# Queries and keys of the windowed heads turned in the projection and stored turned, bias tables built ahead of the global stage

## The chip, the core and the metric

The kernel runs on one core of a Trainium2 chip as one program. The metric is the device time of the whole program in microseconds, as the median of several runs; lower is better. TensorE (PE) multiplies and transposes, VectorE (DVE), ScalarE (ACT) and GpSimd (POOL) do the rest, and SyncE (SP) issues most transfers between memory and the core's SBUF. The engines run their own instruction lists and wait for each other on semaphores.

## What is computed

One encoder layer on x of 2048 rows by 1024, all in float32. Half of the 16 heads (A) attend to the whole sequence, half (B) to a band of 128 positions on each side, with a bias from a table and a learned sink logit. Each half has 8 query heads and 2 key heads of width 64.

```python
h = rmsnorm(x, g_pre_mix)
qa, ka, va, qb, kb, vb = split(h @ w_in)          # 512, 128, 128, 512, 128, 128 columns
out_a = softmax(rope(rmsnorm(qa)) @ rope(rmsnorm(ka)).T / 8) @ va
# for each block of 128 queries of B, over the 384 keys around it:
s = qb @ kb.T / 8 + rel_table[t5_bucket(rel)]     # -1e30 outside the band or the sequence
m = max(max(s), sink)
out_b = exp(s - m) / (sum(exp(s - m)) + exp(sink - m)) @ vb
x = x + rmsnorm(concat(out_a, out_b) @ w_o, g_post_mix)
x = x + rmsnorm(relu(rmsnorm(x, g_pre_ffn) @ w_up) ** 2 @ w_down, g_post_ffn)
```

## The kernel before

Six stages follow each other, and no instruction of one begins before all engines have left the one before: `project`, `attend_global`, `attend_window`, `mix_heads`, `ffn_up`, `ffn_down`. The change touches the first three. Inside a stage every engine's instructions are written out by hand in the order in which it runs them; that order, the waits on semaphores and the order of issues on each engine's DMA queue set what runs when. Nearly every value is carried as a rounded high part and a rest, so that a product of two of them takes two or three passes; a query or key of width 64 therefore fills 128 columns, high and low.

`project` walks 16 tiles of 128 rows. For a tile, TensorE does three chunks of 512 columns (`chunk`, 24 products each), turns the next tile's normalised x behind the first (`turn`), and behind the third turns the ten heads of A of the tile before (`turn_qk`, eight query and two key heads, 128 x 128 each) into one PSUM tile, `qk_ps`. ScalarE evacuates the chunks, copies the turned heads to SBUF (`keep_turned`, L282) and issues stores (`store_qk`, L275 to L277); SP stores the turned heads (`store_turned`). The heads of B are split on VectorE into `q_out` and `k_out` and stored as they are, unturned, to `q_split` and `k_split`. The loop runs over pairs of tiles with the first and the last pair written out (`sweep`).

`attend_global` has 32 blocks (8 heads by 4 chunks of 512 queries) of 8 units each, fully written out. Its start loads queries and keys on SP's queue, computes the row maxima of block 0 in eight pairs of products and three pairs of block 1, and then begins the scores (L766).

`attend_window` has 32 steps, n = 16 query blocks by 2 groups of 4 heads. Its start builds what the steps need. SP loads constants, then the keys in 4 chunks, then the denominators of the global stage (L902, read by VectorE behind the wait of L1099), then queries. TensorE makes an 8 x 512 row of biases (L1119); it goes to memory and comes back as 128 shifted copies (L943, L946, on POOL's queue), and eight products with a flipped identity (L1139), each copied by VectorE (L1069), make the tables `bias`. TensorE also turns the keys, 64 transposes (L1127). In step n it does the four scores of step n + 1 (L1161, L1162, two PSUM banks taken in turn), turns the eight query operands of step n + 2 (L1150, L1151, copied by ScalarE in L1013 and L1014), turns the probabilities (L1169, 12 transposes), folds an output and weighs the values. VectorE adds bias and takes the maximum for each of four heads (L1078), with a one-column copy that nothing reads ahead of each (L1077), and subtracts the rounded probabilities from the exact ones (L1087) after ScalarE has evicted them (L1028). The steps are a `sweep` with two pairs written out in front.

## Time and profile before

| | |
|---|---|
| median of 3 runs | 2890.35 us (2888.19 to 2890.84) |
| the profiled execution | 2890.22 us, of it 2888.6 us span |
| projection | from 0 to about 338.7 us |
| global stage | to about 1051 us |
| window stage | to about 1292 us |
| rest | to 2888.6 us |
| busy, share of the span | PE 94%, DVE 63%, ACT 49%, POOL 28% |
| mean granted clock of TensorE | 0.972 of full speed |

The page of the profile gives busy times and shares of one execution. A timeline row is one instruction or a merged run of equal ones: start, duration, engine, line, operation, output and inputs, shape, count, and in brackets how long the engine had been idle and what ended that. An engine name with a q behind it is the engine's sequencer issuing a transfer; its duration is that of the issue, not of the transfer. TensorE's durations include the time through the array, so rows of one run overlap, and the pace is read from start to start.

### The profile page before, as it was taken

What the parts mean: (1) busy time and instruction counts of PE and PEld (TensorE: products, weight loads), DVE (VectorE), ACT (ScalarE), POOL (GpSimd) and SP (SyncE); (2) the same over time, 40 slices, a digit from 0 to 9 for tenths busy, and PEclk for the clock granted to TensorE, in tenths of its full rate; (3) what the DMA queues carried; (4) which work ended last, traced back from release to release, by engine and by line L of the source; (5) the groups of instructions that cost most, each with busy time, mean ns of one, the idle gap of its engine ahead of it and who ended that gap; (6) DMA issues with size and microseconds to landing.
All of it is one profiled execution on the core that took longest, in us unless ns stands there. A gap on an engine that the chain in (4) does not pass through costs nothing. (4 is left out here: it accounts for less than half of the span.)

```text
span 2888.6 us, 36041 instructions
## 1 busy us (share of the span) xinstructions
PE 2705.4 (94%) x12274; PEld 2185.6 (76%) x12274; DVE 1827.9 (63%) x2503; ACT 1429.2 (49%) x2122; POOL 803.3 (28%) x603
## 2 busy tenths in 40 slices
PE   7999599999999978988995999999998999999998
PEld 5888467777777747976874888788886888888887
DVE  5666499999999947865556666675653343343433
ACT  3222177777777747973334544554443333233332
POOL 1111178888888854541110000000000000000000
PEclk9999799999999989998997999999999999999999
DMA  5333421111111122327876333533325445355442
GB/s 181 107 108 102 122 67 30 31 34 28 35 30 32 23 75 70 84 67 218 207 202 216 124 117 97 209 107 100 114 92 189 171 172 182 121 196 179 172 172 98
DMA packets 295611, 338.16 MB, mean 117 GB/s; under 512 B 73059, under 2 KB 219635, under 8 KB 293292
## 3 DMA queue, kind: packets, MB, share of 16 engines
q1 hardware_dynamic: 269980, 317.92, 35.7%
q10 hardware_dynamic: 23552, 13.64, 1.5%
q0 software_dynamic: 1936, 4.74, 0.6%
q8 instruction: 84, 1.38, 0.2%
q14 instruction: 59, 0.48, 0.0%
HBM read 234.10 MB, written 97.86 MB: 115 GB/s over the span
## 5 line engine op out<-in xcount | busy, mean ns | idle before, releaser
L126 PE MATMUL d_pr<-d_w_hi,d_s_hi 128*128 128x512 f32 x1024 | 399.7, 390 | 11.6 <-DVE d_s_lo L1872 11.6
L1871 DVE TENSOR_TENSOR d_w_lo<-d_w_raw,d_w_hi 128x1024 fp32r<-128x1024 f32 x128 | 156.8, 1225 | 386.2 <-ACT d_s_hi L1848 382.3
L127 PE MATMUL d_pr<-d_w_lo,d_s_hi 128*128 128x512 f32 x1024 | 399.5, 390 | 0.0
L128 PE MATMUL d_pr<-d_w_hi,d_s_lo 128*128 128x512 f32 x1024 | 399.3, 390 | 0.0
L644 POOL TENSOR_TENSOR p_sum<-p_sum,p_hi 128x1024 f32<-128x1024 f32 x160 | 383.3, 2396 | 37.0 <-issue 19.7
L126 PE MATMUL u_pr<-u_t_hi,u_w_hi 128*128 128x512 f32 x896 | 351.2, 392 | 32.3 <-DVE u_t_lo L1687 31.9
L127 PE MATMUL u_pr<-u_t_lo,u_w_hi 128*128 128x512 f32 x896 | 350.1, 391 | 0.0
L128 PE MATMUL u_pr<-u_t_hi,u_w_lo 128*128 128x512 f32 x896 | 350.1, 391 | 0.0
L676 ACT ACTIVATE p_hi<-s_ps 128x1024 fp32r<-128x1024 f32 x256 | 263.3, 1028 | 157.0 <-PE s_ps L767 155.7
L720 DVE TENSOR_TENSOR p_lo<-s_ps,p_hi 128x1024 fp32r<-128x1024 f32 x256 | 312.5, 1221 | 29.5 <-ACT s_ps L677 22.3
L704 DVE TENSOR_REDUCE part_max<-m_ps 128x1 f32<-128x1024 f32 x251 | 304.6, 1214 | 33.1 <-PE m_ps L749 32.9
L1846 ACT ACTIVATE d_w_hi<-d_w_raw 128x1024 fp32r<-128x1024 f32 x128 | 135.6, 1060 | 271.0 <-PE d_pr L128 181.3
L677 ACT ACTIVATE s_ps<-s_ps 128x1024 f32<-128x1024 f32 x256 | 261.4, 1021 | 0.0
L766 PE MATMUL s_ps<-q_all,kt 128*128 128x512 f32 x512 | 219.1, 428 | 18.3 <-DVE p_lo L720 18.2
L126 PEld LDWEIGHTS d_pr<-d_w_hi,d_s_hi 128*128 128x128 f32 x1024 | 192.9, 188 | 52.2 <-DVE d_s_lo L1872 12.1
L128 PEld LDWEIGHTS d_pr<-d_w_hi,d_s_lo 128*128 128x128 f32 x1024 | 193.0, 188 | 40.2
L127 PEld LDWEIGHTS d_pr<-d_w_lo,d_s_hi 128*128 128x128 f32 x1024 | 193.0, 188 | 40.0
L126 PEld LDWEIGHTS u_pr<-u_t_hi,u_w_hi 128*128 128x128 f32 x896 | 169.2, 189 | 70.4 <-issue 34.4
L1630 ACT ACTIVATE u_pr<-u_pr 128x512 f32<-128x512 f32 x128 | 74.5, 582 | 273.4 <-DVE u_pr L1716 126.7
L767 PE MATMUL s_ps<-q_max,kt 65*128 65x512 f32 x512 | 203.9, 398 | 0.0
L1839 POOL TENSOR_TENSOR d_rstd<-d_var,d_half 128x1 f32<-128x1 f32 x16 | 8.8, 550 | 699.7 <-DVE d_var L1879 699.7
L127 PEld LDWEIGHTS u_pr<-u_t_lo,u_w_hi 128*128 128x128 f32 x896 | 169.3, 189 | 35.2
(219 smaller groups left out, 5384.5 us busy)
## 6 DMA issues: line engine op xcount, KB each, us to landing
d_w_raw<-in_w_ffn_down SPq DMA_DIRECT2D x128, 512.0 KB, 3.8
u_w_raw<-in_w_ffn_up SPq DMA_DIRECT2D x32, 1024.0 KB, 6.0
act_blocks<-u_s_out SPq DMA_DIRECT2D x128, 256.0 KB, 6.2
d_s_lo<-act_blocks SPq DMA_DIRECT2D x128, 256.0 KB, 2.7
u_t_lo<-h_blocks SPq DMA_DIRECT2D x14, 1024.0 KB, 10.9
x_in<-in_x SPq DMA_DIRECT2D x16, 512.0 KB, 4.3
q_split<-q_out ACTq DMA_DIRECT2D x16, 512.0 KB, 3.3
q_turned<-w_raw SPq DMA_DIRECT2D x16, 512.0 KB, 3.4
```

Of the source, the lines that this page charges most:

```text
L126: nc.tensor.matmul(out, stat_hi, mov_hi, start=first, stop=False)
L127: nc.tensor.matmul(out, stat_hi, mov_lo, start=False, stop=False)
L128: return nc.tensor.matmul(out, stat_lo, mov_hi, start=False, stop=last)
L644: nc.gpsimd.tensor_tensor(p_sum[:, s], first, p_hi[:, (UNITS * n + u) % SLOTS].bitcast(F32), ALU.add).then_inc(added, 1)
L676: nc.scalar.activation(p_hi[:, slot], scored, ACT.Exp).then_inc(p_hi_ready, 1)
L677: nc.scalar.activation(scored, scored, ACT.Exp).then_inc(probs_ready, 1)
L704: nc.vector.tensor_reduce(part_max[:, m // (PAIRS // QT), m % (PAIRS // QT):m % (PAIRS // QT) + 1], products.rearrange("p b c -> p (b c)") ...
L720: nc.vector.tensor_tensor(p_lo[:, slot], scored, p_hi[:, slot].bitcast(F32), ALU.subtract).then_inc(p_lo_ready, 1)
L766: nc.tensor.matmul(bank, kt[:, g, 0, keys], q_all[:, n % QS], start=True, stop=False)
L767: last = nc.tensor.matmul(bank, kt[0:HD + 1, g, 1, keys], q_max[0:HD + 1, n % QS], start=False, stop=True)
L1846: nc.scalar.activation(w_hi[:, n % SLOTS], w_raw[:, n % RAW], ACT.Copy)
L1871: nc.vector.tensor_tensor(w_lo[:, n % SLOTS], w_raw[:, n % RAW], w_hi[:, n % SLOTS].bitcast(F32), ALU.subtract)
```

## The change

In `project`, the heads of B go into `qkb_out`, of the same form as `qk_out`, and are turned, copied and stored like those of A, by a second call of `turn_qk`, `keep_turned` and `store_turned`; the turned tensors in memory have all 16 heads. `attend_global` gets the making of the bias row and tables, now with the two output banks, and stores the tables to memory. `attend_window` loads turned keys and queries straight into the operand tiles (queries in four slots), and the tables from memory; the turns, their copies, and the one-column copy are gone, and its steps are all written out.

```diff
+        qkb_out = sb("qkb_out", [P, 2, 10, 2 * HD])
+        qkb_t = sb("qkb_t", [P, 2, 10, P])
...
             def store_turned(t, s):
-                sp.wait_ge(qk_kept, t + 1)
-                sp.dma_start(q_cols[t], qk_t[:, s, 0:8]).then_inc(qk_stored[s], 16)
-                sp.dma_start(k_cols[t], qk_t[:, s, 8:10]).then_inc(qk_stored[s], 16)
+                for b, turned in enumerate((qk_t, qkb_t)):
+                    sp.wait_ge(qk_kept, 2 * t + b + 1)
+                    sp.dma_start(q_cols[t][:, 8 * b:8 * b + 8], turned[:, s, 0:8]).then_inc(qk_stored[s], 16)
+                    sp.dma_start(k_cols[t][:, NG * b:NG * b + NG], turned[:, s, 8:10]).then_inc(qk_stored[s], 16)
...
                 act.wait_ge(post_done, t + 1)
-                act.dma_start(scratch["q"].rearrange("(h t) p c -> t p h c", t=NT)[t], q_out[:, s]).then_inc(stored[s], 16)
-                act.dma_start(scratch["k"][t], k_out[:, s]).then_inc(stored[s], 16)
                 act.dma_start(scratch["v_glob"][t], v_out[:, s]).then_inc(stored[s], 16)
...
+                if not (isinstance(t, int) and t < 2):
+                    keep_turned(t - 2, s, p - 1, 1)
                 evacuate(t, s, p, 1)
...
             for s in range(2):
-                keep_turned(NT - 2 + s, s, NT // 2 - 1)
+                for b in range(2):
+                    keep_turned(NT - 2 + s, s, NT // 2 - 1, b)
...
-            def turn_qk(t, s):
+            def turn_qk(t, s, b):
                 pe.wait_ge(post_done, t + 1)
-                at_least(pe, qk_kept, t)
+                at_least(pe, qk_kept, 2 * t + b)
                 for h in range(10):
-                    last = nc.tensor.transpose(qk_ps[:, h], qk_out[:, s, h], ident[:])
+                    last = nc.tensor.transpose(qk_ps[:, h], (qk_out, qkb_out)[b][:, s, h], ident[:])
...
+                if not (isinstance(t, int) and t < 2):
+                    turn_qk(t - 2, s, 1)
                 chunk(t, s, 1)
                 chunk(t, s, 2)
-                turn_qk(t - 1, 1 - s)
+                turn_qk(t - 1, 1 - s, 0)
 
             sweep(pe, NT // 2, tile)
-            turn_qk(NT - 1, 1)
+            turn_qk(NT - 2, 0, 1)
+            for b in range(2):
+                turn_qk(NT - 1, 1, b)
...
             load_q(2)
+            sp.wait_ge(row_ready, 1)
+            sp.dma_start(scratch["bias_row"], bias_row[:]).then_inc(row_moved, 16)
+            sp.wait_ge(row_moved, 16)
+            rows = scratch["bias_row"]
+            sp.dma_start(bias_rev[:], bass.AP(tensor=rows.tensor, offset=rows.offset, ap=[[1, P], [512, 8], [1, SPAN]])).then_inc(row_moved, 16)
             place_max(0)
...
+            pe.wait_ge(row_moved, 32)
+            pe.wait_ge(row_ready, 1)
+            for h in range(8):
+                at_least(pe, bias_ready, h - 1)
+                nc.tensor.matmul((oa_ps, ob_ps)[h % 2][:, 0:SPAN], flip[:], bias_rev[:, h], start=True, stop=True).then_inc(bias_product, 1)
+            pe.wait_ge(bias_ready, 8)
+            pe.wait_ge(filled, 4)
             for n in range(TOTAL):
...
+            load_q(0)
+            load_k(0)
+            sp.dma_start(sink[:], a["sink_b"].to_broadcast([P, 8])).then_inc(const_in, 16)
+            load_bias(0)
             sp.dma_start(ident[:], a["ident"]).then_inc(const_in, 16)
...
+            load_q(1)
+            load_bias(1)
+            load_q(2)
+            load_k(1)
+            load_k(2)
+            load_k(3)
             for j in range(2):
                 sp.dma_start(den[:, j], scratch["den"][j].rearrange("n (t q) -> (n t) q", q=P)).then_inc(den_loaded, 16)
...
-                    nc.vector.tensor_copy(mark[:, h:h + 1], sink[:, head:head + 1])
                     nc.vector.tensor_tensor_reduce(probs[:, s, h], s_ps[:, h % 2, 0:SPAN], bias[:, head], 1.0,
...
                         scores(n + 1, 1 - s, b + s, h)
-                    if h == 0 and not known(n, TOTAL - 2):
-                        turn_q(n + 2, s, b + 1)
                     if h:
                         turn_probs(n, s, h - 1)
```

How the instructions stand. TensorE in the projection's loop, around the turn of the next x; `xt` is the turned x, `qk_ps` the PSUM tile of the turned heads, `pj` the chunks. Before:

```order
L128 MATMUL pj<-w_hi,xt_lo 128x512
L421 REGISTER_ALU
L424 MATMUL xt<-ident,xn 128x128 x8
L59 REGISTER_ALU
L126 MATMUL pj<-w_hi,xt_hi 128x512
L127 MATMUL pj<-w_lo,xt_hi 128x512
```

and now:

```order
L110 MATMUL pj<-w_hi,xt_lo 128x512
L407 REGISTER_ALU
L410 MATMUL xt<-ident,xn 128x128 x8
L59 ISA
L426 MATMUL qk_ps<-ident,qkb_out 128x128 x10
L59 REGISTER_ALU
L108 MATMUL pj<-w_hi,xt_hi 128x512
L109 MATMUL pj<-w_lo,xt_hi 128x512
```

A second group of ten transposes stands between the turned x and the second chunk. SP at the start of the window stage, before:

```order
L895 DMA w_ident<-in_ident 128x128
L896 DMA flip<-in_flip 128x128
L897 DMA onehot<-in_bucket_onehot 33x512
L898 DMA table<-in_rel_bias 32x8
L899 DMA sink<-in_sink_b 128x8
L94 DMA wk_in<-k_split 128x4x128 x8
L902 DMA w_g_den<-den 128x128 x2
L907 DMA wq_in<-q_split 128x4x128 x2
```

and now (`wq_all`, `wq_one` and `wkt` are the operand tiles of queries and keys, `w_g_den` the denominators):

```order
L927 DMA bias<-bias_tables 128x1536
L923 DMA wq_all<-q_turned 128x4x128
L923 DMA wq_one<-q_turned 64x4x128
L914 DMA wkt<-k_turned 64x2x512 x2
L915 DMA wkt<-k_turned 64x2x512
L914 DMA wkt<-k_turned 64x2x512 x2
L915 DMA wkt<-k_turned 64x2x512
L914 DMA wkt<-k_turned 64x2x512 x2
L915 DMA wkt<-k_turned 64x2x512
L941 DMA w_g_den<-den 128x128 x2
L943 DMA rden<-w_g_rden 128x128
```

Ahead of this piece stand eight issues more: query block 0 (two), the first keys (three), the sinks, the first half of the tables and the identity, and behind those the two of query block 1. The denominators, once behind 13 issues of constants and unturned keys, now stand behind 22 of keys, queries and tables. TensorE at the start of the global stage, now, from the last three pairs of products for the maxima (`m_ps`) to the first scores (`s_ps`); before, the scores followed the row of `m_ps` directly:

```order
L766 MATMUL m_ps<-kt,q_all 128x512 x6
L826 MATMUL oa_ps<-bias_rev,flip 128x384
L826 MATMUL ob_ps<-bias_rev,flip 128x384
L826 MATMUL oa_ps<-bias_rev,flip 128x384
L826 MATMUL ob_ps<-bias_rev,flip 128x384
L826 MATMUL oa_ps<-bias_rev,flip 128x384
L826 MATMUL ob_ps<-bias_rev,flip 128x384
L826 MATMUL oa_ps<-bias_rev,flip 128x384
L826 MATMUL ob_ps<-bias_rev,flip 128x384
L783 MATMUL s_ps<-q_all,kt 128x512
```

## Rows read from the trace of the kernel before

**Rows 1.** Busy time by stretch: us, then PE, PEld, DVE, ACT, POOL, clock, DMA share, GB/s.

```profile
39.00:341.00 302.00, 279.42 (x1352) 233.85 (x1352) 187.64 (x348) 78.77 (x137) 54.29 (x31) 0.96 0.35 106
...
1100.00:1293.00 193.00, 184.87 (x1295) 164.18 (x1293) 158.05 (x457) 167.30 (x401) 103.68 (x187) 1.00 0.29 74
```

**Rows 2.** Timeline of TensorE in the projection's loop, around one group of ten transposes.

```profile
300.19 0.39 PE L128 MATMUL pj<-w_hi,xt_lo 128*128 128x512 f32 x1
...
300.42 1.25 PE L440 MATMUL qk_ps<-ident,qk_out 128*128 128x128 f32 x10
...
301.43 0.48 PE L126 MATMUL pj<-w_hi,xt_hi 128*128 128x512 f32 x1
```

**Rows 3.** Timeline of the end of the projection: ScalarE's issues and copies, TensorE's last turns.

```profile
327.15 0.39 ACTq L275 DMA_DIRECT2D q_split<-q_out  x1
...
328.21 1.16 ACTq L277 DMA_DIRECT2D v_glob<-v_out  x1
329.47 1.24 ACT L282 ACTIVATE w_raw<-qk_ps 128x1280 f32<-128x1280 f32 x1 [10.74 <-issue]
...
330.85 2.37 PE L440 MATMUL qk_ps<-ident,qk_out 128*128 128x128 f32 x10 [11.72 <-ACT w_raw L282]
...
333.25 1.24 ACT L282 ACTIVATE w_raw<-qk_ps 128x1280 f32<-128x1280 f32 x1 [2.55 <-PE qk_ps L440]
```

**Rows 4.** Timeline of the start of the global stage: SP's issue, TensorE.

```profile
343.62 7.96 SPq L549 DMA_DIRECT2D q_all<-q_turned  x1
...
363.97 1.19 PE L749 MATMUL m_ps<-kt,q_all 128*128 128x512 f32 x2 [1.41 <-DVE part_max L704]
...
364.96 0.63 PE L766 MATMUL s_ps<-q_all,kt 128*128 128x512 f32 x1
```

**Rows 5.** Table transfer (page, DMA issues) and timeline of the table products and copies.

```profile
bias_rev<-bias_row POOLq DMA_DIRECT2D x1, 1536.0 KB, 7.0
...
1075.62 6.14 PE L1139 MATMUL w_ptp<-bias_rev,flip 128*128 128x384 f32 x16
...
1081.15 1.20 DVE L1069 COPY bias<-w_ptp 128x384 f32<-128x384 f32 x2 [0.36 <-PE w_ptp L1139]
```

**Rows 6.** Timeline of the start of the window stage.

```profile
1051.89 0.36 SPq L895 DMA_DIRECT2D w_ident<-in_ident  x1
...
1090.59 0.28 DVE L1100 TENSOR_TENSOR w_g_den_sum<-w_g_den 128x128 f32<-128x128 f32 x1
...
1091.83 0.61 DVE L1078 CUSTOM_DVE_ANT_0 wprobs<-w_s,bias,sink 128x384 f32<-128x384 f32 x1
...
1100.36 1.46 ACT L1028 ACTIVATE w_pt_hi<-w_ptp 128x1536 fp32r<-128x1536 f32 x1 [1.99 <-PE w_ptp L1169]
```

**Rows 7.** Busy time by stretch, columns as in Rows 1, while loads run.

```profile
340.00:342.00 2.00, 0.00 (x0) 0.00 (x0) 0.00 (x0) 0.00 (x0) 2.00 (x1) 0.50 0.79 168
...
344.00:346.00 2.00, 0.00 (x0) 0.00 (x0) 0.00 (x0) 0.00 (x0) 0.99 (x5) 0.50 1.01 225
...
1060.00:1062.00 2.00, 2.00 (x11) 1.77 (x10) 0.50 (x2) 0.60 (x1) 0.13 (x1) 0.50 1.19 297
...
1068.00:1070.00 2.00, 1.50 (x12) 1.02 (x10) 1.03 (x2) 0.60 (x1) 0.00 (x0) 1.00 0.98 369
```

**Rows 8.** Timeline of the last steps of the window stage, VectorE and TensorE.

```profile
1267.43 1.76 DVE L1087 TENSOR_TENSOR w_pt_lo<-w_ptp,w_pt_hi 128x1536 fp32r<-128x1536 f32 x1
...
1273.35 1.76 DVE L1087 TENSOR_TENSOR w_pt_lo<-w_ptp,w_pt_hi 128x1536 fp32r<-128x1536 f32 x1 [0.22 <-ACT w_pt_hi L1028]
1275.03 0.14 DVE L1077 COPY w_mark<-sink 128x1 f32<-128x1 f32 x1
1275.09 0.61 DVE L1078 CUSTOM_DVE_ANT_0 wprobs<-w_s,bias,sink 128x384 f32<-128x384 f32 x1
...
1279.23 1.76 DVE L1087 TENSOR_TENSOR w_pt_lo<-w_ptp,w_pt_hi 128x1536 fp32r<-128x1536 f32 x1 [0.22 <-ACT w_pt_hi L1028]
...
1275.17 0.55 PE L1169 MATMUL w_ptp<-w_ident,wprobs 128*128 128x128 f32 x3 [0.35 <-DVE w_pt_lo L1087]
```

More of the change, by code:

```diff
@@ new lines, in load_q, with load_bias @@
+            def load_q(n):
+                at_least(sp, scores_done, GRP * (n - QS + 1))
+                b, g = n // NG, n % NG
+                heads = slice(8 + GRP * g, 8 + GRP * (g + 1))
+                dest = (q_all[:, n % QS], q_one[0:HD, n % QS])
+                for tile, rows in zip(dest, (slice(0, 2 * HD), slice(HD, 2 * HD))):
+                    sp.dma_start(tile.bitcast(F32).rearrange("p (h c) -> p h c", h=GRP), q_cols[b][rows, heads]).then_inc(q_loaded[n % QS], 16)
+            def load_bias(g):
+                heads = slice(GRP * g, GRP * (g + 1))
+                sp.dma_start(bias[:, heads], scratch["bias"][:, heads]).then_inc(bias_in[g], 16)
@@ L909, in _ @@
-            for g in range(NG):
-                load_q(0, g)
             sp.wait_ge(den_inverted, 1)
@@ L919, in step @@
             def step(n, g, b):
-                if not known(n, TOTAL - 2):
-                    load_q(b + 1, g)
+                if n + 3 < TOTAL:
+                    load_q(n + 3)
                 if not (isinstance(n, int) and n < 4):
                     store(n - 4, b - 2, g)
-            sweep(sp, NT, step, 2)
+            every(sp, NT, step)
             for n in range(TOTAL - 4, TOTAL):
@@ L994, in step @@
                     load_v(b + 1, s)
-            sweep(pool, NT, step, 2)
+            every(pool, NT, step)
             denominator(TOTAL - 1, 1)
@@ L1046, in step @@
                     exponentials(n + 1, 1 - s)
-            sweep(act, NT, step, 2)
+            every(act, NT, step)
             keep_o(TOTAL - 2, 0)
@@ L1109, in step @@
                 low(n, s)
-            sweep(dve, NT, step, 2)
+            every(dve, NT, step)
             finish(TOTAL - 2, 0, NT - 1)
@@ L1212, in step @@
                     weigh(n - 1, 1 - s)
-            sweep(pe, NT, step, 2)
+            every(pe, NT, step)
             turn_o(TOTAL - 2, 0)
```

227 lines of the change are left out of this document (79 added, 148 removed).

## The prediction

> **What bounds the kernel now.** I read the busy time of the stages first, then the timeline at the seams between them, then one step of the window stage. From 39 to 341 us, the projection, TensorE is busy 279.42 of 302.00 us, and in the window stage 184.87 of 193.00 [rows 1]; VectorE and ScalarE have room in the first and less of it in the second. In the projection the reader should see ten transposes standing between two runs of products with no idle time ahead of them: they start at 300.42, the next product at 301.43 and it takes 0.48 instead of 0.39 [rows 2]. So one group of ten costs 1.01 + 0.09 = 1.10 us of a chain that never stops. At the seams TensorE stands still: at the end of the projection it waits for ScalarE's copies [rows 3], at the start of the window stage for keys, tables and one query load [rows 6]. In the running window step the question is whether TensorE or a chain through three engines sets the period; this decides whether taking its query turns away is worth anything.
>
> **Part 1, the projection's loop: +15.4 us.** Each tile gets a second group of ten transposes. For tiles 0 to 13 these stand behind the first chunk of a later tile, 14 groups at 1.10 us [rows 2], and nothing in that loop idles TensorE, so all of it lies on the path. What goes away there (two of ScalarE's three stores a tile) and what comes (a second copy of 1.24 us a tile, two more issues on SP) lies beside it: ScalarE is busy 78.77 of 302 us [rows 1]. Bounds: 0 if some wait absorbed it, for which no row speaks, and 15.4.
>
> **Part 2, the projection's end: +6.5 us.** Before, ScalarE issues its last three stores, the last from 328.21, then copies (329.47), TensorE turns the last tile (330.85, 2.37 us at the lower clock), and ScalarE copies again (333.25 to 334.49) [rows 3]. One copy-and-turn round is 333.25 - 329.47 = 3.78 us. After the change one store is left of three; it is issued about 1.06 us earlier (328.21 - 327.15, the time at which the first one stands in the rows), so the copies begin at 328.4. But there are now four copies with three turns between them, each waiting for the other because the turned heads share one PSUM tile: 328.4 + 3 x 3.78 + 1.24 = 341.0 against 334.5. If the clock came back in the later rounds, a turn would take the 1.25 us of [rows 2] and the end would be about 2.2 us earlier: bounds 4.3 and 6.5. I take 6.5, since TensorE idles 1.4 of every 3.8 us there.
>
> **Part 3, the global stage's start: +7.8 us.** The small product and its copy lie under the loading of the keys, for which TensorE waits anyway. The 1.5 MB table transfer does not: SP can issue the row only behind the third query load, whose issue lasts from 343.62 to 351.58 [rows 4], it must then wait for the row to land, and the transfer took 7.0 us to land before [rows 5]. That puts the tables in SBUF at about 364 to 366. TensorE finishes its eleven pairs of products at 363.97 + 1.19 = 365.16 [rows 4], so up to here it is nearly hidden. The eight products and copies are not: from 1075.62 to 1081.15 + 1.20 = 1082.35 they took 6.7 us [rows 5], they now stand ahead of the first scores, and their first copy must wait for VectorE's reduction of the last pair, for which TensorE waits 1.41 us ahead of the product at 363.97 [rows 4]; I take 1.2 us. 365.2 + 1.2 + 5.9 = 372.3 and 0.4 us to the first score's start, against 364.96: +7.8. Bounds: +5.5 if the clock comes back during the tables and spares the slow first products that follow now; +11 if the row or the tables land 3 us later. The store of the finished tables and SP's wait for them come when the next query load is still many units away from being needed; nothing for them.
>
> **Part 4, the window stage's start: -17.5 us.** The stage begins at 1051.89, and the first eviction of turned probabilities, which needs a whole first step, starts at 1100.36 [rows 6]. Key turns, table products and query turns between them disappear. What is late next? The first scores need about 2 MB and should start near 1061. But VectorE, after the first block's four heads, waits for the softmax denominators (L1099), and their load now stands on SP's queue behind every key, bias and early query load: 3.15 MB of keys, 1.18 MB of queries, 1.57 MB of tables, 0.2 MB of small ones. I take rates from [rows 7]: 225 GB/s while keys went to 64 partitions, 297 for 512-byte pieces, 369 for the tables. 14.0 + 4.0 + 4.3 + 0.7 = 23.0 us, with some 2 us until the engines are full and 0.3 at the end: 1077.2. From the sum of the denominators to the end of the first head of block 1 it takes 1091.83 + 0.61 - 1090.59 = 1.85 us [rows 6]: 1079.0. From there to the eviction: in a running step the distance from a head's copy to the next VectorE subtraction is 1279.23 - 1275.03 = 4.20 us [rows 8]; without 0.7 for the head and 1.5 for the eviction 2.0 us remain. About 1.7 of that is TensorE's (nine transposes at 0.10 and four products of 384 columns at three quarters of 0.23, both from [rows 2]), which doubles at the lower clock: 3.7 to 3.8. Eviction at 1082.8, 17.5 us earlier. Bounds: everything at 369 GB/s gives 6.8 us more gain, keys at 168 (while the first ones of the global stage came in, [rows 7]) 4.8 us less. The wait for denominators is the new wait here; behind it on VectorE stands all of block 1.
>
> **Part 5, the window's steps: -3.0 us.** TensorE looks full, and eight query turns a step go. But the kernel before contains a step without them. The subtractions stand at 1267.43, 1273.35 and 1279.23 [rows 8]: 5.92 us with turns, 5.88 us without, and in the second TensorE waits 0.35 us for the subtraction (row at 1275.17). So the period belongs to the chain subtraction - first head on VectorE - third scores - turns of the probabilities - eviction - subtraction. The removed copy of one column adds 1275.09 - 1275.03 = 0.06 us to that chain once a step, since the copy stands ahead of the first head. 5.82 us a step, 0.10 less, 30 steps: 3.0 us. Bounds: 1.2 us (5.88) to what a TensorE-bound step would give, the first rival. ScalarE's two query copies (1.1 us a step) fall into its idle time before the eviction; their cover was that idle time, so nothing is won.
>
> **Sum.** 15.4 + 6.5 + 7.8 - 17.5 - 3.0 = +9.2 us. The profiled execution took 2890.22 us (span 2888.6), 0.13 below the median of 2890.35; forecast 2899.4 us.
>
> **The rivals.** *TensorE sets the window's period (faster).* Then each step loses its eight turns, 8 x 0.11 = 0.87 us with the delay of the product behind them [rows 2], 26 us instead of 3: 2899.4 - 23 = 2876. For it: TensorE's 184.87 of 193 us, which looks like the bound. Against it: the 5.88 us step. It decides if the chain through VectorE can start earlier once turns are gone; that needs more than 0.3 us a step. *The loads come at the full rate.* The denominators at 1070.4, the clock returning at the projection's end: 2899.4 - 6.8 - 2 = 2891, no difference that can be told. For it: 369 GB/s for tables in [rows 7]; against it: the keys' 225. *The loads are slow.* Keys at 168 GB/s and the global stage's tables 3 us late: 2899.4 + 4.8 + 3 = 2907. For it: many issues ahead of the denominators, and SP's 7.96 us for one issue [rows 4]. *The added turns hide.* If the projection had slack that the rows don't show, Part 1 is zero: 2884.
>
> The Trainium skill bears on the second rival ("DMA: Bandwidth & Descriptors", sections Specifications and "Anatomy of one DMA"): about 2.0 us fixed plus bytes over the rate, with some 358 GB/s as one core's share of memory. By that, 5.97 MB are there 18.7 us after the issue, at 1070.6, and the sum would be 2893. The trace doesn't agree with one rate for all: 369 GB/s is above that limit, and 225 far below it.
>
> **How the numbers follow.** Forecast 0.50, steps bound by TensorE 0.11, full-rate loads 0.22, slow loads 0.12, hidden turns 0.05. The forecast's own bounds are 2893 to 2905. The range 2888 to 2908 leaves out the first and last rival on the fast side (0.16) and a little above. A measurement of this kernel can tell about 0.2% (5.8 us) from no change. Slower by more than that, above 2896.1: 0.62 (the forecast and the slow loads). Within: 0.22. Faster, below 2884.6: 0.16.
>
> **What would show it.** In the profile after: a tile of the projection 1.10 us longer than before; four copies from the transposes' PSUM tile at the projection's end, 3.8 us apart; eight table products ahead of the first scores of the global stage and those scores some 8 us further from the stage's start; VectorE idle for about 10 us before the denominators' sum, ended by their DMA; the subtractions of the window stage 5.8 us apart. I would be wrong first of all if these stand 5.1 us apart, or if VectorE doesn't wait for the denominators.

## The result and the profile after

The changed kernel takes 2906.03 us (median of 5 runs, 2902.15 to 2907.04) against 2890.35 us (2888.19 to 2892.11) before: ratio 1.0051, with a 95% interval of 1.0037 to 1.0066. Slower by 15.7 us, where 9.2 were forecast. Between the two profiled executions the cost came in at 29.8 us (29.7 forecast) and the gain at 16.0 us (20.5 forecast); 2.9 us more lie in stages that the change doesn't touch.

SyncE's first load of each stage divides the executions. Its timeline before, for the two places that the rows ahead don't show:

```profile
338.76 0.36 SPq L549 DMA_DIRECT2D q_all<-q_turned  x1
...
1292.71 0.36 SPq L1295 DMA_DIRECT2D m_ident<-in_ident  x1
```

and after, for the global, the window and the mix stage:

```profile
359.29 0.36 SPq L548 DMA_DIRECT2D q_all<-q_turned  x1
...
1081.74 0.41 SPq L923 DMA_DIRECT2D wq_all<-q_turned  x1
...
1306.52 0.35 SPq L1245 DMA_DIRECT2D m_ident<-in_ident  x1
```

The reader takes the stages' lengths from these starts, [rows 6] and the spans (2888.6 and 2905.3 us). The same reading for every kernel of this study, in us ("times" are medians; the ratio is to the kernel before on the same chip):

| kernel | projection | global | window | the rest | span | time | ratio |
|---|---|---|---|---|---|---|---|
| before | 338.8 | 713.1 | 240.8 | 1595.9 | 2888.6 | 2890.35 | |
| after | 359.3 | 722.4 | 224.8 | 1598.8 | 2905.3 | 2906.03 | 1.0051 |
| after_again | 359.6 | 724.5 | 226.8 | 1594.1 | 2905.0 | 2906.47 | 1.0048 |
| before_extra_turns | 353.9 | 713.9 | 240.5 | 1597.3 | 2905.6 | 2907.22 | 1.0051 |
| tail_banks | 352.2 | 722.4 | 225.7 | 1593.9 | 2894.1 | 2895.67 | 1.0019 |
| late_tables | 360.7 | 720.5 | 224.7 | 1594.4 | 2900.3 | 2902.16 | 1.0039 |
| den_early | 359.8 | 724.6 | 213.4 | 1592.3 | 2890.1 | 2891.76 | 1.0007 |
| keys_later | 358.7 | 723.9 | 218.1 | 1593.9 | 2894.6 | 2898.18 | 1.0026 |
| window_filler | 358.9 | 724.0 | 225.8 | 1595.6 | 2904.4 | 2906.31 | 1.0051 |
| after_with_mark | 359.3 | 724.2 | 226.3 | 1592.7 | 2902.5 | 2903.91 | 1.0051 |
| three_slots | 359.1 | 720.8 | 216.8 | 1595.8 | 2892.4 | 2897.94 | 1.0030 |
| turns_together | 359.2 | 723.4 | 205.4 | 1596.7 | 2884.6 | 2885.84 | 0.9975 |
| combined | 352.9 | 719.8 | 199.5 | 1593.7 | 2865.8 | 2865.66 | 0.9911 |
| combined_keys_later | 352.9 | 717.7 | 202.8 | 1595.7 | 2869.2 | 2866.47 | 0.9919 |

From before to after: projection +20.5, global stage +9.3, window stage -16.0, rest +2.9, together 16.7 us between the profiled executions. The rest runs the same instructions in all rows of the table and lies anywhere from 1592.3 to 1598.8: it is scatter. A single stage's row is good to some 2 us, which is why the experiments below are read at the place that their edit touches, and in the whole time only second. The mean over all executions that run the same instructions in a stage (nine of the projection and of the global stage after, four of the window stage after; one of the projection before and two of the other two stages) gives +20.6, +9.8 and -15.2 us, together 15.2: the difference of the medians, with nothing left for the rest.

**The projection.** The timeline of TensorE in the loop, the rows that answer to [rows 2]:

```profile
300.99 0.39 PE L110 MATMUL pj<-w_hi,xt_lo 128*128 128x512 f32 x1
...
302.10 1.25 PE L426 MATMUL qk_ps<-ident,qkb_out 128*128 128x128 f32 x10
303.11 0.48 PE L108 MATMUL pj<-w_hi,xt_hi 128*128 128x512 f32 x1
```

The new group of ten takes 1.01 us to the next product and delays that by 0.09, as the old one did. Its end, by VectorE's last subtraction, ScalarE's store and copies, and one of TensorE's turns (to be set beside [rows 3]):

```profile
341.65 0.29 DVE L353 TENSOR_TENSOR qk_out<-rot,qk_out 128x128 f32<-128x128 f32 x1
...
341.97 0.34 ACTq L259 DMA_DIRECT2D v_glob<-w_raw  x1
342.41 1.24 ACT L264 ACTIVATE w_raw<-qk_ps 128x1280 f32<-128x1280 f32 x1 [8.88 <-DVE qk_out L353]
346.19 1.24 ACT L264 ACTIVATE qkb_t<-qk_ps 128x1280 f32<-128x1280 f32 x1 [2.55 <-PE qk_ps L426]
349.98 1.24 ACT L264 ACTIVATE w_raw<-qk_ps 128x1280 f32<-128x1280 f32 x1 [2.55 <-PE qk_ps L426]
353.77 1.24 ACT L264 ACTIVATE qkb_t<-qk_ps 128x1280 f32<-128x1280 f32 x1 [2.55 <-PE qk_ps L426]
...
347.58 2.37 PE L426 MATMUL qk_ps<-ident,qk_out 128*128 128x128 f32 x10 [1.42 <-ACT qkb_t L264]
```

Four copies 3.78 us apart, each waiting for a turn, each turn for the copy before it. The last copy ends at 355.01, 20.5 us later than at 334.49.

**The global stage's start.** TensorE's last pair of maxima products, the first and fifth table product, VectorE's last table copy and the first scores, and beside them the busy time with the granted clock (columns as in [rows 1]):

```profile
384.99 1.19 PE L766 MATMUL m_ps<-kt,q_all 128*128 128x512 f32 x2 [1.41 <-DVE part_max L716]
386.00 1.65 PE L826 MATMUL oa_ps<-bias_rev,flip 128*128 128x384 f32 x2
387.44 1.49 PE L826 MATMUL ob_ps<-bias_rev,flip 128*128 128x384 f32 x2
...
391.28 0.82 PE L826 MATMUL oa_ps<-bias_rev,flip 128*128 128x384 f32 x2
...
394.62 0.56 DVE L742 COPY g_bias<-ob_ps 128x384 f32<-128x384 f32 x1 [0.36 <-PE ob_ps L826]
...
395.23 0.50 PE L783 MATMUL s_ps<-q_all,kt 128*128 128x512 f32 x1 [0.65 <-DVE g_bias L742]
...
384.00:390.00 6.00, 5.01 (x8) 2.59 (x9) 3.18 (x4) 0.00 (x0) 0.00 (x0) 0.50 0.11 22
```

The first scores stand 35.9 us behind the stage's first load, 26.2 before (364.96 in [rows 4] less 338.76). The tables' stretch, 386.00 to 395.18, is 9.2 us long.

**The window stage's start.** VectorE's sum of the denominators, ScalarE's first eviction, the first two subtractions, and the busy time while the loads run and in the first step:

```profile
1109.82 0.29 DVE L1088 TENSOR_TENSOR w_g_den_sum<-w_g_den 128x128 f32<-128x128 f32 x1 [10.97 <-DMA w_g_den<-den]
...
1115.16 1.45 ACT L1029 ACTIVATE w_pt_hi<-w_ptp 128x1536 fp32r<-128x1536 f32 x1 [13.68 <-PE w_ptp L1123]
...
1116.65 1.76 DVE L1075 TENSOR_TENSOR w_pt_lo<-w_ptp,w_pt_hi 128x1536 fp32r<-128x1536 f32 x1 [1.79 <-ACT w_pt_hi L1029]
...
1123.75 1.76 DVE L1075 TENSOR_TENSOR w_pt_lo<-w_ptp,w_pt_hi 128x1536 fp32r<-128x1536 f32 x1 [1.53 <-ACT w_pt_hi L1029]
...
1084.00:1108.00 24.00, 5.72 (x15) 3.81 (x15) 7.78 (x14) 2.60 (x9) 2.50 (x5) 0.50 1.00 251
1110.00:1123.00 13.00, 8.73 (x38) 7.68 (x39) 7.71 (x21) 4.67 (x11) 4.01 (x8) 0.68 0.46 115
```

The new wait is where it was forecast, 10.97 us for the denominators. The eviction comes 33.4 us after the stage's first load, 48.5 before [rows 6]; the second subtraction 7.10 us after the first.

**The steps.** One step of the running stage, TensorE's turn, ScalarE's eviction, VectorE's subtractions, and the busy time of 24 steps:

```profile
1240.46 1.76 DVE L1075 TENSOR_TENSOR w_pt_lo<-w_ptp,w_pt_hi 128x1536 fp32r<-128x1536 f32 x1 [0.22 <-ACT w_pt_hi L1029]
...
1242.27 0.55 PE L1123 MATMUL w_ptp<-w_ident,wprobs 128*128 128x128 f32 x3 [0.35 <-DVE w_pt_lo L1075]
...
1244.81 1.45 ACT L1029 ACTIVATE w_pt_hi<-w_ptp 128x1536 fp32r<-128x1536 f32 x1 [1.42 <-PE w_ptp L1123]
...
1246.29 1.76 DVE L1075 TENSOR_TENSOR w_pt_lo<-w_ptp,w_pt_hi 128x1536 fp32r<-128x1536 f32 x1 [0.22 <-ACT w_pt_hi L1029]
...
1130.00:1270.00 140.00, 131.63 (x817) 106.77 (x816) 112.20 (x265) 105.97 (x266) 80.33 (x144) 1.00 0.41 108
```

5.83 us a step, with TensorE waiting for the subtraction in each. Every engine has idle time: the step is a ring of waits, not a full engine. The same stretch of the kernel before:

```profile
1130.00:1270.00 140.00, 140.00 (x995) 126.34 (x994) 121.06 (x353) 127.89 (x310) 77.99 (x142) 1.00 0.31 81
```

There TensorE never stops. Its own instructions fill the 5.92 us of a step, and neither a product nor a weight load of it waits for another engine in these 140 us. The step without turns in [rows 8] takes 5.88 us and has a wait of 0.35 us.

### The profile page after: what moved, and what is told of

Read it like the earlier page. It is cut to its first block and busy times, and to the rows that moved or that the text cites. A ratio compares the mean times of both kernels' runs of the same rounds, so it can differ in the third digit from the quotient of the medians.

```text
span 2905.3 us, 34682 instructions
## 1 busy us (share of the span) xinstructions
PE 2700.0 (93%) x12114; PEld 2168.7 (75%) x12114; DVE 1816.2 (63%) x2367; ACT 1411.0 (49%) x2066; POOL 797.7 (27%) x598
## 5 line engine op out<-in xcount | busy, mean ns | idle before, releaser
L110 PEld LDWEIGHTS u_pr<-u_t_hi,u_w_lo 128*128 128x128 f32 x896 | 169.1, 189 | 35.5
```

Of the source, the lines that this page charges most:

```text
L110: return nc.tensor.matmul(out, stat_lo, mov_hi, start=False, stop=last)
```

## The experiments

The theory is the forecast's: five separate terms, of which the projection's are TensorE's time and one shared PSUM tile, the window's start is the denominators behind the other loads, and the window's steps are a chain. The rivals are named with each run.

**The base again.** No edit.

> The kernel after, unchanged, as the base of the other three of this group on the same chip. The stages behind the window stage, which the change doesn't touch, took from 1592.3 to 1598.8 us in six profiled executions, and 1598.8 in the one of after. Theory (2.9 of the 16.7 us by which the two profiled executions differ are this scatter, not the change): the median lies at 2902 to 2905 us, ratio to before 1.004 to 1.005, and the part in front of the mix stage's first load is again 13.8 us longer than before's, within 1 us. Rival (the change costs the later stages 3 us): 2905 to 2908 us.

2906.47 us (2903.96 to 2907.16), ratio 1.0048 (1.0034 to 1.0061). The time was not lower, and the mix stage's first load stood 18.2 us later than before's, not 13.8: in this execution the scatter lay in the global and window stages and the rest was short (1594.1). So both numbers of the theory missed. The time lies in the rival's range, but not by its mechanism: the later stages cost nothing by themselves. One pair of profiles doesn't split 15 us to the microsecond. The difference of 15 to 16 us is firm.

**The projection's loop by itself**, in the kernel before:

```
+                if not (isinstance(t, int) and t < 2):
+                    at_least(pe, qk_kept, t - 1)
+                    for h in range(10):
+                        nc.tensor.transpose(qk_ps[:, 10 + h % 2], ident[:], ident[:])
                 chunk(t, s, 1)
```

> The kernel before, with ten transposes of the identity, into two unused slots of the turned heads' PSUM tile, in each of tiles 2 to 15 of the projection, where the kernel after turns the local heads; nothing else changes: no copies, no stores, no queues. Theory (the loop's cost is TensorE's time alone): VectorE's last split comes 14 to 15.4 us later than in before and the kernel takes 14 to 16 us more, 2904 to 2906. Rival (the turns hide, and the projection of after is longer for its copies and stores): 0 to 4 us more.

2907.22 us, ratio 1.0051 (1.0038 to 1.0065), 15.9 us more. VectorE's last subtraction, which stood at 326.83 in the kernel before:

```profile
342.01 0.29 DVE L368 TENSOR_TENSOR qk_out<-rot,qk_out 128x128 f32<-128x128 f32 x1
```

15.2 us for 14 groups, 1.08 each, with no copy, store or queue changed. The loop's cost is TensorE's time alone, and the rival that the turns hide has fallen.

**The projection's end on two PSUM tiles:**

```
-            turn_qk(NT - 2, 0, 1)
-            for b in range(2):
-                turn_qk(NT - 1, 1, b)
+            pj_heads = pj[:].rearrange("p b (h c) -> p (b h) c", c=P)
+            pe.wait_ge(evacuated, 3 * NT)
+            turn_qk(NT - 2, 0, 1, pj_heads)
+            turn_qk(NT - 1, 1, 0, qk_ps)
+            turn_qk(NT - 1, 1, 1, pj_heads)
```

(Cut: `turn_qk` gets the tile as an argument, and its wait for ScalarE's copies is one copy looser.) ScalarE copies both groups of tile 14 ahead of its last store.

> The kernel after, with the projection's last turns alternating between two PSUM tiles (the turned heads' and that of the projection's products, free by then), and ScalarE's copies of tile 14 ahead of its last store. Theory (the end is longer because four copies and three turns wait for each other over one PSUM tile, 3.78 us a round): the four copies no longer stand 3.8 us apart, ScalarE's last one ends about 348 instead of 355.0, and the kernel takes 6 to 7 us less, about 2899. Rival (the low clock and the stores' landing set the end): the copies move together, but the global stage starts less than 3 us earlier, 2903 or more.

2895.67 us, ratio 1.0019 (1.0010 to 1.0028). ScalarE's last two copies:

```profile
344.31 1.24 ACT L265 ACTIVATE w_raw<-qk_ps 128x1280 f32<-128x1280 f32 x1 [7.58 <-PE qk_ps L429]
346.37 1.24 ACT L265 ACTIVATE qkb_t<-pj 128x1280 f32<-128x1280 f32 x1 [0.82 <-PE pj L429]
```

The last ends at 347.61 and the global stage begins at 352.2, 7.1 us earlier than in after, as the theory said; the time fell by 10.4, 3 more than the edit explains. The turns were as slow as before (2.3 to 2.4 us, the lower clock), so overlapping them with the copies is enough to shorten the end; what a full clock would give there wasn't run.

**The tables at the global stage's end:**

```
+                    if n == TOTAL - 1:
+                        if u == 0:
+                            pe.wait_ge(row_moved, 32)
+                            pe.wait_ge(max_reduced, PAIRS * TOTAL)
+                        at_least(pe, bias_ready, u - 1)
+                        nc.tensor.matmul(m_ps[:, u % 2, 0:SPAN], flip[:], bias_rev[:, u], start=True, stop=True).then_inc(bias_product, 1)
```

> The kernel after, with the bias tables' eight products and copies placed one by one in the eight units of the global stage's last iteration, where the PSUM tile of the maxima is free and TensorE waits 0.5 us in every second unit, the table transfer issued in the third iteration, and the small product behind the first eleven pairs of products. Theory (the tables cost 9.7 us at the start: 1.0 by a late first product and 8.7 ahead of the first scores): the first scores come 9 us earlier against the stage's start, of which the small product there takes 0.5 to 1; in the last iteration the eight products cost 0 to 5 us; in all 4 to 8 us less, about 2900. Rival (what the tables took was given back at once by a warm clock, so that it was nearly free): less than 2 us, 2904 or more.

2902.16 us (2899.56 to 2902.72), ratio 1.0039 (1.0026 to 1.0053): 3.9 us less, below the 4 to 8 expected and above the rival's 2. At the start the small product and the first scores, and near the end one of the eight products:

```profile
387.83 1.87 PE L822 MATMUL ob_ps<-onehot,table 33*8 33x512 f32 x2
389.63 0.79 PE L784 MATMUL s_ps<-q_all,kt 128*128 128x512 f32 x1
...
1060.03 0.81 PE L836 MATMUL m_ps<-bias_rev,flip 128*128 128x384 f32 x2
1060.38 0.92 PE L799 MATMUL oa_ps<-p_hi,v 128*128 128x512 f32 x2
```

The first scores come 29.0 us after the stage's first load instead of 35.9. The small product, 1.80 us from start to start at the lower clock, now stands in their way. Each table product costs 0.35 us and 0.29 us at the product behind it, 5 us in eight units. The tables are thus worth 7 us at the start, 9 with the small product, and TensorE had little room for them elsewhere.

**The denominators' load on ScalarE's queue:**

```
@@ SyncE, behind load_k(3)
-            for j in range(2):
-                sp.dma_start(den[:, j], ...).then_inc(den_loaded, 16)
@@ ScalarE, ahead of exponentials(0, 0)
+            for j in range(2):
+                act.dma_start(den[:, j], ...).then_inc(den_loaded, 16)
```

> The kernel after, with the two loads of the global stage's denominators issued by ScalarE as its first instructions of the window stage instead of by SyncE behind 22 other issues. Theory (the denominators' load is the new wait of the window stage's start): VectorE's wait of 10.97 us ahead of their sum falls to under 1 us, the first eviction of turned probabilities comes 9 to 11 us earlier against the stage's first load, and the kernel takes about 2896 us against 2906 (ratio to before about 1.002). Rival (the second block's queries and tables, which stand in the same queue, come almost as late): a new wait takes over most of it, the gain is 0 to 4 us, 2902 to 2906.

2891.76 us, ratio 1.0007 (0.9998 to 1.0016). VectorE's sum and the first eviction:

```profile
1101.08 0.29 DVE L1088 TENSOR_TENSOR w_g_den_sum<-w_g_den 128x128 f32<-128x128 f32 x1
...
1106.03 1.45 ACT L1027 ACTIVATE w_pt_hi<-w_ptp 128x1536 fp32r<-128x1536 f32 x1 [2.23 <-PE w_ptp L1123]
```

No wait ahead of the sum is left, and the eviction comes 21.7 us after the stage's first load (1084.34) instead of 33.4. The window stage is 213.4 us long, 11 to 13 shorter than in the four kernels whose window stage is that of after. The time fell by 14.3 us by the medians (12.7 by the ratios), where 10 were expected. The gain at the place of the edit, 11.7 us, is the wait of 10.97; it alone was worth most of what the change lost.

**Fewer bytes ahead of the denominators,** which stay on SyncE's queue:

```
             load_k(1)
-            load_k(2)
-            load_k(3)
@@ step
+                if n in (2, 5):
+                    load_k(2 + n // 5)
```

> The kernel after, with the last two of the four chunks of window keys loaded in steps 2 and 5 of the window stage instead of at its start; the denominators stay on SyncE's queue, behind the rest. Theory (the wait for the denominators is the bytes ahead of them over the rate of this stretch, 6.27 MB in 24 us, 261 GB/s): 1.57 MB less put them 6.0 us earlier, the wait ahead of their sum is 5 to 6 us instead of 11 to 12, and the kernel takes 5 to 6.5 us less than after, about 2900. Rival (they wait for SyncE's issues, 0.6 us each, and for the landing, not for bytes): six issues less put them 3.6 us earlier, about 2902.5.

2898.18 us, ratio 1.0026 (1.0016 to 1.0036), 8 us less than after and a little more than the 5 to 6.5 expected.

```profile
1103.82 0.29 DVE L1088 TENSOR_TENSOR w_g_den_sum<-w_g_den 128x128 f32<-128x128 f32 x1 [4.12 <-DMA w_g_den<-den]
```

The sum stands 21.2 us behind the stage's first load (1082.61), 6.9 us earlier than in after, and 6.9 less is waited. (The row of after gives 251 GB/s for 1084 to 1108 and not the 261 of the expectation, so 1.57 MB are 6.3 us.) The rival's 3.6 us, issues alone, is too little. The trace of after says the same: SyncE issued the denominators' loads from 1097.93 on, 11.9 us before the sum could start.

**TensorE's turns put back** into the window steps, as transposes of the identity:

```
+                    if h == 0:
+                        for k in range(2 * GRP):
+                            nc.tensor.transpose(tb_ps[:, k % GRP], ident[:], ident[:])
```

> The kernel after, with eight transposes of the identity into a free PSUM bank in each of the window stage's steps, where the kernel before turned its queries. Theory (a chain through VectorE and ScalarE sets the step, and TensorE's turns fall mostly into its wait for the subtraction): the subtractions stand 5.83 to 5.92 us apart instead of 5.83, in all 0 to 3 us more than after. Rival (TensorE sets the step): 0.87 us a step more, 6.7 us apart, 26 us more in all.

2906.31 us. Two subtractions and the filler between them:

```profile
1242.11 1.76 DVE L1076 TENSOR_TENSOR w_pt_lo<-w_ptp,w_pt_hi 128x1536 fp32r<-128x1536 f32 x1 [0.22 <-ACT w_pt_hi L1030]
...
1248.01 1.76 DVE L1076 TENSOR_TENSOR w_pt_lo<-w_ptp,w_pt_hi 128x1536 fp32r<-128x1536 f32 x1 [0.22 <-ACT w_pt_hi L1030]
...
1243.06 1.04 PE L1159 MATMUL w_tb<-w_ident 128*128 128x128 f32 x8
```

5.90 us a step: eight turns of TensorE cost 0.07 us, not 0.87. But they also fill TensorE, as they did before. The busy time in the running stage, and between the first two subtractions:

```profile
1130.00:1270.00 140.00, 140.00 (x1000) 126.50 (x998) 115.17 (x261) 104.58 (x263) 78.97 (x142) 1.00 0.40 106
...
1118.00:1124.00 6.00, 4.58 (x29) 3.53 (x28) 4.25 (x10) 4.10 (x11) 2.48 (x5) 1.00 0.42 106
```

So there are two bounds next to each other. With eight turns TensorE's own work is 5.90 us; without them it is about 5.03 (5.90 less 0.80 from the first turn's start to the next product and 0.07 by which that is slower, an estimate), and the ring of 5.83 sets the step. The rival added the turns' 0.87 us to the ring's 5.83; they belong on TensorE's own 5.03. The turns do something else too: the first two subtractions stand 5.83 us apart here (1118.35 and 1124.18) at the full clock, and 7.10 to 7.44 us in the four kernels whose window stage is that of after. So the turns cost 1.8 us over the later steps and gave 1.3 to 1.6 back in the first.

**The one-column copies put back,** ahead of each head:

```
+                    nc.vector.tensor_copy(mark[:, h:h + 1], sink[:, head:head + 1])
```

> The kernel after, with the copy of one column ahead of each head on VectorE put back. Theory (one of a step's four copies stands in the chain that sets the step, 0.06 us): the subtractions stand 5.89 us apart instead of 5.83, in all 2 us more than after (2908), which the time can hardly tell and the rows can. Rival (all four copies stand in it, since VectorE is full): 6.0 to 6.1 us apart, 5 to 8 us more.

2903.91 us (2903.31 to 2909.05), no difference from after by time. The subtractions stand 5.89 to 5.90 us apart, 0.06 more, and TensorE still waits in each step: one of the four copies is in the ring. The kernel before had both, a ring of 5.89 us with the copies and turns that fill TensorE for 5.90 or more; its 5.92 are the larger of the two and not their sum.

**A third PSUM slot for the scores:**

```
-        s_ps = ps("w_s", [P, 2, NB])
+        s_ps = ps("w_s", [P, 3, NB])
@@ scores; the slot is (GRP * n + h) % 3
-                at_least(pe, biased, GRP * n + h - 1)
+                at_least(pe, biased, GRP * n + h - 2)
```

> The kernel after, with three PSUM slots instead of two for a block's scores, in the bank that the query turns left free. Theory (a chain sets the window's period of 5.83 us: subtraction, first head on VectorE, third head's scores, turns of the probabilities, eviction, subtraction; TensorE does not bound it): the third scores no longer wait for the first head, the chain loses 0.3 to 0.5 us, the subtractions stand 5.3 to 5.5 us apart and the kernel takes 10 to 16 us less, 2890 to 2896. Rival (TensorE's work or the clock sets the period): it stays at 5.8 us and the time at 2906.

2897.94 us, ratio 1.0030 (1.0018 to 1.0042), 8.1 us less, short of the 10 to 16 expected. The subtractions stand 5.58 us apart, short of the 5.3 to 5.5 expected, and TensorE still waits 0.36 us for each: the wait for the first head is gone (the third scores start 0.30 us behind the first turn, 0.54 in after), but two heads' scores still stand between the turns.

**The turns together,** in the kernel three_slots:

```
-                for h in range(GRP):
+                for h in range(GRP - 1):
                     if not known(n, TOTAL - 1):
                         scores(n + 1, 1 - s, b + s, h)
-                    if h:
-                        turn_probs(n, s, h - 1)
-                turn_probs(n, s, GRP - 1)
+                for h in range(GRP):
+                    turn_probs(n, s, h)
+                if not known(n, TOTAL - 1):
+                    scores(n + 1, 1 - s, b + s, GRP - 1)
```

> The kernel three_slots, with TensorE's order in a window step changed: three heads' scores, then all four heads' turns of probabilities, then the last head's scores, instead of scores and turns in alternation. Theory (in three_slots the chain of subtraction, turns and two scores between them, eviction and subtraction sets the step of 5.58 us; without the two scores it is 4.9, and TensorE's own work of 5.22 us sets it): the subtractions stand 5.2 to 5.3 us apart, 9 to 12 us less than three_slots, 2886 to 2889 us. Rival (VectorE is full): 5.5 us or more, less than 3 us gained.

2885.84 us, ratio 0.9975 (0.9966 to 0.9984). Subtractions, and the busy time of the running stage:

```profile
1242.08 1.75 DVE L1075 TENSOR_TENSOR w_pt_lo<-w_ptp,w_pt_hi 128x1536 fp32r<-128x1536 f32 x1
...
1247.32 1.75 DVE L1075 TENSOR_TENSOR w_pt_lo<-w_ptp,w_pt_hi 128x1536 fp32r<-128x1536 f32 x1
...
1130.00:1270.00 140.00, 139.35 (x905) 120.57 (x904) 118.54 (x291) 120.26 (x291) 88.05 (x159) 1.00 0.42 113
```

5.24 us between these two, 5.27 in the mean of the stage. No product of TensorE waits any longer, but it isn't quite a full engine: in each step a weight load waits 0.25 us for ScalarE's last exponential, and ScalarE 0.65 us for GpSimd. Only now does it pay to have taken the queries' turns away, since with them TensorE's own work was 5.90 us a step (this order with the turns wasn't run). VectorE is busy 118.54 of 140 us: the rival has fallen.

**All of them.** The edits of tail_banks, late_tables, den_early and turns_together, with late_tables' small product ahead of the last three pairs of products.

> The edits of den_early, tail_banks, late_tables and turns_together in one kernel; of late_tables the small product stands one place earlier, ahead of the last three pairs of products, where TensorE waits 2.7 us for VectorE. Theory (each removes a separate stretch of the path, so their gains add): the projection's end 7 us earlier, first scores of the global stage 7 to 8.5 us earlier against its start with 5 us given back in its last iteration, no wait for the denominators (11 us), window steps of 5.25 us; 2906 - 7 - 3 - 11 - 20 = 2865 us, ratio to before 0.991, range 2861 to 2870. Rival (what one edit frees another takes back: turns_together already evicts the first block ahead of VectorE's wait, and a window start bound by the keys' loads): 2872 us or more.

2865.66 us (2861.32 to 2868.97), ratio 0.9911 (0.9896 to 0.9926): the fastest kernel here, 25 us below the one before. Against after the projection lost 6.4 us, the global stage 2.7, the window stage 25.3, where the sum had 31: here the rival was right in part. That the time still came out at the 2865 expected is luck: 5.1 us of the difference of the two profiled executions lie in the untouched rest, where after had its longest value. A new wait has taken 6 us: the second and third subtraction stand 11.39 us apart. TensorE at the third block's scores, and GpSimd's issue of a value load and its next operation but one:

```profile
1103.32 0.69 PE L1123 MATMUL w_s<-wkt,wq_all 128*128 128x384 f32 x1 [4.61 <-DMA wq_one<-q_turned]
...
1093.68 0.81 POOL L980 DMA_DIRECT2D wv_in<-v_win  x1
...
1101.90 1.03 POOL L995 TENSOR_TENSOR w_rden<-w_den,w_minus_one 128x4 f32<-128x4 f32 x1 [7.18 <-issue]
```

**All of them, with two key chunks later:** keys in steps 2 and 5 as in keys_later, the fourth query load ahead of the second chunk, the store of the inverted denominators in step 1.

> The kernel combined, with the same two chunks of keys loaded in steps 2 and 5, the fourth query load ahead of the second chunk, and the store of the inverted denominators in step 1. In combined TensorE waits 4.61 us at the third window step for a query load that stands behind all keys, and the second and third subtraction are 11.39 us apart. Theory (the loads' bytes set this wait too): that distance falls to 5.2 to 7 us, the kernel takes 4 to 6 us less than combined, 2860 to 2862 us. Rival (GpSimd, which stood 7.18 us behind its own value load at that place, holds ScalarE's exponentials by itself): less than 2 us, 2864 or more.

2866.47 us (2865.90 to 2870.98), nothing gained. TensorE no longer waits for the queries, but GpSimd stands still as before. A key chunk's issue on SyncE's queue, and GpSimd's power (`w_rden`), whose own value load was issued at 1091.62:

```profile
1091.47 1.89 SPq L922 DMA_DIRECT2D wkt<-k_turned  x2
...
1100.25 1.03 POOL L997 TENSOR_TENSOR w_rden<-w_den,w_minus_one 128x4 f32<-128x4 f32 x1 [7.59 <-issue]
```

The two subtractions are 10.61 us apart (11.39 in combined), and at the later chunk, loaded in step 5, another distance grew to 9.12. The rival was right. Between the sum `w_den` and the power the program has a drain and a wait for an older output of VectorE, and the rows don't name VectorE as what ended the stall. That the drain waits for the value load's work while other loads fill the queues fits the rows, but no kernel without the drain or with the load on another queue was run, so it stays open.

## Why the prediction was right, and where its terms were off

The sign, the order of the terms and the new wait were right, and the time lies in the range of 2888 to 2908. It lies outside the forecast's own bounds of 2893 to 2905, near the 2907 of the rival of slow loads. That rival's mechanism came only in part: the denominators were 2.8 us late where it had 4.8, and the tables cost more through the clock, not by landing late, since their first product follows the last pair without a wait. That the range held to its upper end is partly luck. By its own steps, read in the two profiled executions:

| part | forecast | measured | what was off |
|---|---|---|---|
| 1, the loop | +15.4 | +14.8 | 1.06 us a group instead of 1.10 |
| 2, the end | +6.5 | +5.7 | ScalarE's last store was issued in 0.34 us, not 1.16, so the copies began 0.8 us sooner |
| 3, the tables | +7.8 | +9.3 | eight products at the lower clock |
| 4, the window's start | -17.5 | -15.1, and +1.2 in the first step | loads, and a step not counted |
| 5, the steps | -3.0 | -2.3 | 5.92 to 5.83 us, not 5.82 |

**Parts 1 and 2** rested on rows of the same operations at the same place. before_extra_turns and tail_banks show both mechanisms.

**Part 3.** The failed step is the 5.9 us (behind a first copy's 1.2) taken from [rows 5]. There the granted clock was 1.00:

```profile
1075.60:1079.00 3.40, 3.39 (x11) 1.48 (x10) 2.65 (x5) 0.00 (x0) 0.43 (x1) 1.00 0.24 58
```

At the new place it was 0.50 (1.2 GHz) and the first four products stand 1.28 to 1.44 us apart instead of 0.78; products and copies took 9.2 us instead of 6.7. The forecast had only used the clock as a possible gain (the bound 5.5). From the last pair's product to the first scores 9.25 us more passed than before, where the forecast had 7.8: of the 2.5 us, 1.0 came back because the first table product and the first scores each followed what stood ahead of them sooner than assumed. Another 0.5 us passed ahead of the last pair, and 0.4 was made good behind the first scores; no run isolates these two. The measured value still lies below the upper bound of 11.

**Part 4.** The denominators came 28.1 us after the stage's first load, 25.3 were forecast. The bytes' term was 23.0 us for 6.1 MB, 265 GB/s; the row from 1084 to 1108 shows 251, so 24.3. The remaining 1.5 us are the way from the end of the full DMA engines to VectorE's start, for which 0.3 had been set. Taking a rate for each kind of load was right: by stretches of 2 us, after shows 217, 219 and 185 GB/s from 1084 to 1090, while the first keys came, 369, 308 and 345 from 1090 to 1096, where by the bytes the tables and queries lie, and 193 to 249 from 1096 to 1108, where the other keys do. From the sum to the eviction 5.34 us passed, 5.6 were forecast. Not in the sum at all was the first step: 7.10 us at a granted clock of 0.68, where a step at full clock takes 5.83. Before, the first distance was 5.88: TensorE had turned keys and queries ahead of it and stood at full clock. window_filler, with TensorE at the full clock in that step, has 5.83 again, so it was the clock. keys_later shows that bytes set the landing. The 6.8 us of the full-rate bound were worked from 5.97 MB, where the forecast's own terms add up to 6.10; with these it is 6.5, and nothing hangs on it.

The single rate of the Trainium skill ("DMA: Bandwidth & Descriptors", sections Specifications and "Anatomy of one DMA") gave, as an estimate, 18.7 us for the same loads; after and keys_later, 28.1 us and a saving of 6.9 us for 1.57 MB (228 GB/s), disagree with it, and so the rival of full-rate loads fell. The page's 2.0 us are for a single transfer issued by GpSimd, and its 358 GB/s are a limit of memory, which need not be what a queue of mixed loads reaches; what held these loads below it no run here shows.

**Part 5.** The price was right, the reason only in part. The forecast read the chain off one step without turns [rows 8], against TensorE's 184.87 of 193 us [rows 1], and concluded that the period belongs to the chain. For the running steps of the kernel before that is wrong: TensorE is busy 140.00 of 140 us there and waits for nothing, so its own work is the 5.92 us. What the step without turns did show rightly is the bound behind it, the ring of 5.88, and that is what a step costs once the turns are gone. So the premise of the rival of a TensorE-bound step held and its price of 0.87 us a step fell: window_filler has 5.90 us with the turns, after 5.83 without. three_slots and turns_together show the ring for what it is, since one more PSUM slot and another order of the same instructions shorten the step to 5.58 and 5.24 us.

**The rest** (2.9 us between the profiles) is the stages behind, which vary by 6.5 us over 14 executions of the same instructions there. The means of the stages put none of the difference there: against the forecast they are 1.3 us less in the projection (20.6 for 21.9), 2.0 more in the global stage (9.8 for 7.8) and 5.3 less gain in the window stage (15.2 for 20.5), 6.0 of the 6.5 us by which the time missed. The clock at the tables and in the window's first step and the loads' delay make up most of it.

## What to carry to other kernels

An engine that never idles in a stage is a bound, but taking work off it gains only the distance to the next bound. Here that was 0.09 us for work of 0.87: a ring of waits through three engines lay just under it. Look for one step without the work in question and price the edit from that, as the forecast did; and if a ring is what remains, break it (one more buffer, the loaded operands' work together) before taking work away. A small load that an early instruction needs goes ahead of bulk loads or on another queue; behind 6 MB it cost 11 us, most of the loss. Work that is moved to a stage's start must be priced at the clock of that place: products of 0.78 us at full clock took 1.28 to 1.44 us here in the first four of eight.

## What the runs showed of the hardware

GpSimd's power in a window step usually starts 1.6 to 1.9 us after the operation before it (the medians of eleven executions), with a drain in between and a value load of its own just issued. While the stage's other loads were on their way it stood still far longer there: 7.18 us (combined), 7.59 and 4.68 (combined_keys_later), 7.19 (den_early) and 4.58 (keys_later), with nothing in the trace that it waited for. Stalls of 2.6 to 3.9 us also stand where no keys were loading (window_filler, after_with_mark), so the keys alone don't explain it. The loads at the start of after's window stage came at 251 GB/s together, in stretches of 2 us at 308 to 369 for tables and queries and 185 to 249 for keys into 64 partitions (which load lies in a stretch is told by the order of their bytes). The clock that the tables met had been full a little earlier, as busy time by stretch of after shows:

```profile
376.00:378.00 2.00, 1.15 (x4) 0.31 (x3) 2.00 (x3) 0.66 (x1) 0.00 (x0) 1.00 0.76 208
...
382.00:384.00 2.00, 1.19 (x2) 0.50 (x2) 0.62 (x2) 0.00 (x0) 0.00 (x0) 0.50 1.06 396
```

Between the two TensorE had waited 2.69 us for a reduction of VectorE's (ahead of its pair at 380.27), and the clock was back only in the fifth table product.
